# One cast and one low part for a weight block, in place of two halves of each

## The chip, the cores and the metric

The kernel runs on one NeuronCore of one Trainium2 chip. The metric is the device time of one execution in microseconds (us); the time before is the median of three runs.

## The reference

Two transformer blocks with two layers each, one after the other, on 256 tokens of width 1024, all in fp32. Cut to what matters here:

```python
def token_mixers(x, ...):                       # first block, per layer
    h = x @ w_in                                # 1024 -> 5704 columns, split into 11 parts
    ya = diff_attention(...)                    # 4 heads, two softmaxes each
    yb = dsa_attention(..., topk=64)            # 8 heads over the 64 best keys of an index
    merged = sigmoid(ga) * (ya @ w_bd) + sigmoid(gb) * (yb @ w_bs)
    return merged @ w_o
def first_block(...):
    x = layer_norm(ALPHA * x + mix)
    ffn = hierarchical_moe(x, ...)              # 32 experts, 2 of a group of 8 per token
    x = layer_norm(ALPHA * x + ffn + sigmoid(x @ w_ple_gate) * (p @ w_ple))
def second_block(...):                          # per layer
    x = x + hybrid_mixer(rms_norm(x) @ w_in)    # MLA, MoBA and retention branches
    x = x + square(relu(rms_norm(x) @ w_up)) @ w_down      # 1024 -> 4096 -> 1024
```

## The kernel before

The products outside the experts are made with split operands. Every weight block W (128 partitions by up to 2048 fp32 columns, 1 MB) becomes a pair: hi, which is W rounded to fp32r, and lo = W - hi. TensorE then makes three products for one, hi by hi, hi by lo and lo by hi (`mm3`, L1215, or `mm_both`, L1220). The experts' weights are used raw, with no pair.

A planner (`Plan`, L102) writes one list of steps, and each engine's program walks that same list and issues its own share of every step, in that order. So the order within an engine's queue is the plan's, and an instruction that waits holds up all that stand behind it on its engine. The steps that matter:

- `fetch` (L1186, the sync engine's queue): loads a block into a buffer, one of three ring buffers or one lent by other tiles. Where the buffer held a block that had been split, it waits for that block's low part.
- `split` (planned in `prepare`, L191): the block is made into its pair in one of three pairs of tiles WS (`PAIRS`, L46). ScalarE casts the high part, L2276, in two halves of the columns; before each it waits for the load and for TensorE to have read the pair's last block, three blocks earlier. VectorE makes the low part, L1638, in two halves, each behind its half of the cast. `ahead` (L184) plans a block's split up to two blocks before its use.
- Six of the 218 split blocks are marked "hi" (`low_part`, L570, L459, L557): their casts stay in their place, and each half of the low part is a step of its own further back. These are one in the second attention, one ahead of the first layer norm and one after the last expert, in each layer of the first block.
- `wide`, `gate`, `branch`, `mlp_up`, `mlp_down` and the like use one block each. TensorE waits for its whole low part (`lo_done`) and for a free PSUM bank; four banks go round, and ScalarE or VectorE frees each by an eviction or an addition. Such evictions are L2307 (ScalarE), L1837 and L1917 (VectorE). L2307 stands behind the casts in ScalarE's queue, L1837 and L1917 behind the low parts in VectorE's.

The steps around the prediction's places: `attend` (L315) orders an attention, whose scores L1794 to L1798 (VectorE) and exponentials L2334 (ScalarE) are mixed with blocks; `turn` (L251, TensorE's L1311) transposes heads; `turn_p` (L356, TensorE's L1382) transposes probabilities; `index` steps (L1771 to L1781) pick the 64 best keys on VectorE between the low parts; `route` steps on VectorE and ScalarE pick the experts and end in the mask MK (L2065), from which `ranks` (L1445) counts on TensorE. In the second block `rms`, `normed` and `wide` begin a layer, and `mlp_up` is relu, square and a correction that goes over VectorE (L2210), ScalarE (L2524, L2527), GpSimd (L2595) and VectorE (L2214).

Of the kernel before, what the change touches and what calls it, by code (L numbers as in the profile page):

```python
# [818 lines left out]
def build(nc, plan, table, wts, rows, cols, consts, pos, x0, x0T, pT, out):  # L819

    ctx = ExitStack()
    with ctx:
# [746 lines left out]
        def blocks_free(m):  # L1569

            return plan.split_block[m - PAIRS] if m >= PAIRS else None

        @block.vector
        def vector_program(e):
# [51 lines left out]
            for s in plan.steps:  # L1626
                l, i, u, t = s.l, s.i, s.u, s.t
                if s.kind == "split" and s.c != "hi":
                    hi, lo = WS[s.m % PAIRS]
                    buf = buffers[s.buffer]  # L1630
                    for k in range(2) if s.c is None else [s.c]:
                        c = slice(k * (s.n // 2), s.n // 2 if k == 0 else s.n)
                        dve.wait_ge(hi_done, "half", i, k)
                        if blocks_free(s.m) is not None:
                            dve.wait_ge(pe_done, "read", blocks_free(s.m))
                        if s.m in plan.also:
                            dve.wait_ge(pe_done, *plan.also[s.m])
                        nc.vector.tensor_tensor(lo[:, c], buf[:, c], hi[:, c].bitcast(F32), ALU.subtract).then_inc(  # L1638
                            *lo_done.inc(("block", i)))
# [225 lines left out]
                elif s.kind in ("turn_split", "shifted_split"):  # L1865
                    hi, lo = (v[:, 2 * s.j:2 * s.j + s.n, :] for v in SPLIT[s.name][0])
                    names = [(s.name, l, s.j)] + ([("x", l + 1, s.j)] if s.name == "ln2" else [("attn", l, s.j)] if s.name == "at0" else [])
                    if s.name in SHIFTED:
                        scale, bias = SHIFTED[s.name]
                        Y = (TMP, TMP2)[s.j % 2][:, 0:s.n * S]  # L1870
                        if s.kind == "turn_split":
# [6 lines left out]
                            for k in range(s.n):  # L1878
                                c = 2 * s.j + k
# [121 lines left out]
                elif s.kind == "route":  # L2001
# [51 lines left out]
                    elif n in (25, 27):  # L2053
                        c = (n - 25) // 2
                        nc.vector.tensor_tensor(val[:, c, t:t + 1], r_["m9"][:, c:c + 1], r_["es"], ALU.mult).then_inc(*dve_done.inc(name))
                    else:
                        c = (n - 26) // 2
# [191 lines left out]
        def scalar_program(e):  # L2249
# [15 lines left out]
            for s in plan.steps:  # L2265
                l, i, u, t = s.l, s.i, s.u, s.t
                if s.kind == "split" and s.c in (None, "hi"):
                    hi = WS[s.m % PAIRS][0]
                    for k in range(2):
                        c = slice(k * (s.n // 2), s.n // 2 if k == 0 else s.n)  # L2270
                        act.wait_ge(landed[s.buffer], "block", i)
                        if blocks_free(s.m) is not None:
                            act.wait_ge(pe_done, "read", blocks_free(s.m))
                        if s.m in plan.also:
                            act.wait_ge(pe_done, *plan.also[s.m])
                        nc.scalar.copy(hi[:, c], buffers[s.buffer][:, c]).then_inc(*hi_done.inc(("half", i, k)))  # L2276
# [83 lines left out]
                elif s.kind in ("turn_split", "shifted_split"):  # L2360
                    hi = SPLIT[s.name][0][0][:, 2 * s.j:2 * s.j + s.n, :]
                    name = (s.name, l, s.j)
                    if s.name in SHIFTED:
# [4 lines left out]
                        if s.kind == "turn_split":  # L2368
# [6 lines left out]
                            for k in range(s.n):  # L2375
                                c = 2 * s.j + k
# [298 lines left out]
```

## Time and profile before

| | |
|---|---|
| median of three runs | 1809.89 us (1809.01 to 1810.49) |
| profiled execution | 1810.35 us, span 1808.5 us |
| TensorE busy | 1776.3 us, 98% |
| VectorE busy | 1120.0 us, 62%, 2063 instructions |
| ScalarE busy | 860.5 us, 48%, 1515 instructions |
| low parts, L1638, out of the ring buffers | 460.7 us in 404 instructions |
| casts, L2276, out of the ring buffers | 390.3 us in 404 instructions |
| granted TensorE clock | 0.996 of full speed |

The profile is of one execution; the span runs from its first to its last instruction. A row of a timeline has the start, the duration, the engine, the line, the operation, the tile written and the tiles read with their sizes, and how many instructions are merged into the row; in square brackets is how long the engine was idle before it and what ended that. PE is TensorE, DVE VectorE, ACT ScalarE. WSh and WSl are the high and the low part of a block. Durations of neighbours overlap a little.

### The profile page before, as it was taken

What the parts mean: (1) busy time and instruction counts of PE and PEld (TensorE: products, weight loads), DVE (VectorE), ACT (ScalarE), POOL (GpSimd) and SP (SyncE); (2) the same over time, 40 slices, a digit from 0 to 9 for tenths busy, and PEclk for the clock granted to TensorE, in tenths of its full rate; (3) what the DMA queues carried; (4) which work ended last, traced back from release to release, by engine and by line L of the source; (5) the groups of instructions that cost most, each with busy time, mean ns of one, the idle gap of its engine ahead of it and who ended that gap; (6) DMA issues with size and microseconds to landing.
All of it is one profiled execution on the core that took longest, in us unless ns stands there. A gap on an engine that the chain in (4) does not pass through costs nothing.

```text
span 1808.5 us, 28658 instructions
## 1 busy us (share of the span) xinstructions
PE 1776.3 (98%) x11788; PEld 1444.6 (80%) x11788; DVE 1120.0 (62%) x2063; ACT 860.5 (48%) x1515; POOL 68.9 (4%) x79
## 2 busy tenths in 40 slices
PE   9999999999899999999989999999999999999998
PEld 8889975555688999555558899988888899988887
DVE  6986863233678777423347776775557577675555
ACT  5565542232545546223235655455554565455554
POOL 2000000000000000000000000001100000000001
PEclk9999999999999999999999999999999999999999
DMA  8427589999543576999975433545554533355552
GB/s 304 167 108 298 196 318 420 420 421 421 221 167 118 211 303 214 421 421 421 420 295 192 140 139 142 180 169 190 196 192 157 198 136 141 140 186 186 190 195 82
DMA packets 61083, 426.66 MB, mean 236 GB/s; under 512 B 6976, under 2 KB 7120, under 8 KB 11920
## 3 DMA queue, kind: packets, MB, share of 16 engines
q1 hardware_dynamic: 59760, 421.65, 61.3%
q8 instruction: 96, 1.57, 0.3%
q0 software_dynamic: 464, 1.89, 0.3%
q10 hardware_dynamic: 720, 1.19, 0.2%
q14 instruction: 43, 0.35, 0.1%
HBM read 423.66 MB, written 1.05 MB: 235 GB/s over the span
## 4 chain that ended last, share of the span: by engine, by line
PE 82%; DVE 12%; ACT 4%; issue 1%; POOL 1%; DMA 0%; DVEq 0%; POOLq 0%
PE bank L1213 64%; PE scp L1213 14%; DVE WSl L1638 4%; ACT SC L2334 2%; PE bank L1502 1%; DVE sm L1796 1%; PE bank L1343 1%; PE bank L1311 1%; DVE scp L1794 1%; ACT WSh L2276 1%; POOL sm L2549 1%; PE bank L1382 1%; DVE TMP L1781 0%; DVE sm L1587 0%; DMA A<-x0T 0%
## 5 line engine op out<-in xcount | busy, mean ns | idle before, releaser
L1638 DVE TENSOR_TENSOR WSl<-ring,WSh 128x1024 fp32r<-128x1024 f32 (+4 forms) x404 | 460.7, 1183 | 147.5 <-ACT WSh L2276 147.1
L2276 ACT CAST WSh<-ring 128x1024 fp32r<-128x1024 f32 (+4 forms) x404 | 390.3, 1020 | 160.6 <-PE scp L1213 80.4
L1213 PE MATMUL bank<-XB,WSh 128*128 128x256 f32 (+1 forms) x1920 | 433.1, 314 | 0.0
L1213 PE MATMUL bank<-XB,WSl 128*128 128x256 f32 x1216 | 331.7, 281 | 0.0
L1213 PEld LDWEIGHTS bank<-XB,WSh 128*128 128x128 f32 x1920 | 311.3, 191 | 19.4 <-issue 0.9
L1213 PE MATMUL bank<-WSh,XB 128*128 128x512 f32 (+4 forms) x1088 | 312.8, 367 | 5.3 <-DVE WSl L1638 3.6
L1213 PEld LDWEIGHTS bank<-XB,WSl 128*128 128x128 f32 x1216 | 231.5, 190 | 6.5 <-DVE XB L1902 0.6
L1213 PEld LDWEIGHTS bank<-WSh,XB 128*128 128x128 f32 x1088 | 199.2, 189 | 35.8 <-DVE WSl L1638 5.0
L1213 PE MATMUL bank<-WSl,XB 128*128 128x512 f32 (+4 forms) x544 | 198.7, 365 | 0.0
L1213 PE MATMUL scp<-WSh,FA 128*128 128x512 f32 x512 | 159.1, 389 | 0.0
L1213 PE MATMUL bank<-FA,WSh 128*128 128x256 f32 x640 | 116.6, 284 | 0.7 <-DVE FA L1846 0.7
L2152 DVE TENSOR_SCALAR WSl<-O,CST 128x256 fp32r<-128x256 f32 x64 | 22.3, 349 | 150.6 <-PE scp L1213 150.6
L1213 PEld LDWEIGHTS bank<-WSl,XB 128*128 128x128 f32 x544 | 102.9, 189 | 13.3
L1213 PEld LDWEIGHTS scp<-WSh,FA 128*128 128x128 f32 x512 | 96.1, 188 | 19.7
L2479 ACT COPY WSF<-bank 128x256 f32<-128x256 f32 x64 | 23.9, 373 | 171.9 <-PE bank L1213 171.9
L1213 PEld LDWEIGHTS bank<-FA,WSh 128*128 128x128 f32 x640 | 99.6, 192 | 1.7 <-issue 1.7
L1213 PE MATMUL scp<-WSl,FA 128*128 128x512 f32 x256 | 99.6, 389 | 0.0
L1213 PE MATMUL bank<-WSh,FA 128*128 128x512 f32 (+1 forms) x336 | 94.8, 365 | 0.0
L1213 PE MATMUL bank<-FA,WSl 128*128 128x256 f32 x320 | 90.5, 283 | 0.0
L1213 PE MATMUL bank<-A,WSF 128*64 128x256 f32 x672 | 76.4, 381 | 0.0
L2334 ACT ACTIVATE SC<-scp,sm 128x256 f32<-128x256 f32 (+1 forms) x128 | 52.2, 420 | 49.6 <-DVE sm L1798 48.9
L2549 POOL TENSOR_TENSOR sm<-sm,CST 128x1 f32<-128x1 f32 (+1 forms) x30 | 23.3, 780 | 1233.7 <-DVE sm L1606 1015.5
(325 smaller groups left out, 2445.2 us busy)
## 6 DMA issues: line engine op xcount, KB each, us to landing
ring<-wts SPq DMA_DIRECT2D x220, 1024.0 KB, 4.8
A<-wts SPq DMA_DIRECT2D x64, 1024.0 KB, 14.4
V<-wts SPq DMA_DIRECT2D x28, 1024.0 KB, 15.8
WSF<-wts SPq DMA_DIRECT2D x20, 1024.0 KB, 16.7
SC<-wts SPq DMA_DIRECT2D x16, 1024.0 KB, 16.0
PT<-wts SPq DMA_DIRECT2D x14, 1024.0 KB, 16.2
H<-wts SPq DMA_DIRECT2D x12, 1024.0 KB, 17.5
FAF<-wts SPq DMA_DIRECT2D x8, 1024.0 KB, 10.6
```

The lines of the kernel that those rows point to most:

```text
L1213: return nc.tensor.matmul(dst, lhsT, rhs, start=start, stop=stop)
L1311: last = nc.tensor.transpose(bank[u % 4][0:s.w, j * P:(j + 1) * P], src, ident)
L1343: last = nc.tensor.transpose(bank[u % 4][:, j * P:(j + 1) * P], src(t, c), ident)
L1382: last = nc.tensor.transpose(bank[u % 4][:, (j - s.first) * P:(j - s.first + 1) * P], p_at(j // nk)[:, j % nk * P:(j % nk + 1) * P], ident)
L1502: last = nc.tensor.transpose(bank[u % 4][:, f * P:(f + 1) * P], SE[s.e % 2][:, f * P:(f + 1) * P], ident)
L1638: nc.vector.tensor_tensor(lo[:, c], buf[:, c], hi[:, c].bitcast(F32), ALU.subtract).then_inc(*lo_done.inc(("block", i)))
L1794: nc.vector.tensor_tensor(v, v, mask.unsqueeze(1).broadcast_to([P, 4, kl - m0]), ALU.add).then_inc(*dve_done.inc())
L2152: nc.vector.tensor_scalar(ct, SR[:, 0, :], sid, None, ALU.is_equal).then_inc(*dve_done.inc())
L2276: nc.scalar.copy(hi[:, c], buffers[s.buffer][:, c]).then_inc(*hi_done.inc(("half", i, k)))
L2334: ins = nc.scalar.activation(SC[:, h, 0:kl], scp[:, h, 0:kl], ACT.Exp, bias=nb[t][:, h:h + 1], scale=SCALE[s.name], accum_out=zs[t][:, h:h ...
L2479: nc.scalar.copy(SE[s.e % 2], bank[u % 4][:, 0:DE]).then_inc(*act_done.inc(("bank", u), ("SE", l, s.e)))
L2549: nc.gpsimd.tensor_tensor(var, var, const("nhalf")[:, 0:groups], ALU.pow).then_inc(*pool_done.inc(("pow", *name)))
```

## The change

Where a split is not marked, one cast covers all columns of the block and one low part follows it. The signal that is left is that of the second half, k = 1. Marked splits keep their halves.

```diff
@@ vector_program
                 if s.kind == "split" and s.c != "hi":
                     hi, lo = WS[s.m % PAIRS]
                     buf = buffers[s.buffer]
-                    for k in range(2) if s.c is None else [s.c]:
-                        c = slice(k * (s.n // 2), s.n // 2 if k == 0 else s.n)
+                    for k in [1] if s.c is None else [s.c]:
+                        c = slice(0, s.n) if s.c is None else slice(k * (s.n // 2), s.n // 2 if k == 0 else s.n)
                         dve.wait_ge(hi_done, "half", i, k)
@@ scalar_program
                 if s.kind == "split" and s.c in (None, "hi"):
                     hi = WS[s.m % PAIRS][0]
-                    for k in range(2):
-                        c = slice(k * (s.n // 2), s.n // 2 if k == 0 else s.n)
+                    for k in [1] if s.c is None else range(2):
+                        c = slice(0, s.n) if s.c is None else slice(k * (s.n // 2), s.n // 2 if k == 0 else s.n)
                         act.wait_ge(landed[s.buffer], "block", i)
```

## Rows read from the trace of the kernel before

**Rows 1.** The page's busy time: us, share of the span, instructions.
```profile
PE 1776.3 (98%) x11788; PEld 1444.6 (80%) x11788; DVE 1120.0 (62%) x2063; ACT 860.5 (48%) x1515; POOL 68.9 (4%) x79
```

**Rows 2.** Groups by line and form: busy us, mean ns | idle before, releaser.
```profile
L2276 ACT CAST WSh<-ring 128x1024 fp32r<-128x1024 f32 x360 | 359.3, 1053 | 145.8 <-PE scp L1213 73.2 <-PE bank L1213 69.9 <-DMA ring<-wts 2.7
...
L2276 ACT CAST WSh<-ring 128x512 fp32r<-128x512 f32 x4 | 2.3, 618 | 5.6 <-PE bank L1213 5.6
...
L1638 DVE TENSOR_TENSOR WSl<-ring,WSh 128x1024 fp32r<-128x1024 f32 x360 | 424.9, 1223 | 135.4 <-ACT WSh L2276 135.2
...
L1638 DVE TENSOR_TENSOR WSl<-ring,WSh 128x512 fp32r<-128x512 f32 x4 | 2.6, 688 | 4.5 <-ACT WSh L2276 4.5
```

**Rows 3.** Timeline of 60 to 95 us: start us, us, engine, line.
```profile
63.74 1.99 ACT L2276 CAST WSh<-ring 128x1024 fp32r<-128x1024 f32 x2
...
64.81 2.36 DVE L1638 TENSOR_TENSOR WSl<-ring,WSh 128x1024 fp32r<-128x1024 f32 x2 [0.46 <-ACT WSh L2276]
...
84.47 1.99 ACT L2276 CAST WSh<-ring 128x1024 fp32r<-128x1024 f32 x2
...
85.67 2.35 DVE L1638 TENSOR_TENSOR WSl<-ring,WSh 128x1024 fp32r<-128x1024 f32 x2
...
92.15 1.97 PE L1311 MATMUL bank<-CST,A 128*128 128x128 f32 x16 [0.71 <-DVE A L1837]
```

**Rows 4.** Timeline of 128 to 152 us.
```profile
128.25 2.01 ACT L2276 CAST WSh<-ring 128x1024 fp32r<-128x1024 f32 x2
...
129.34 2.36 DVE L1638 TENSOR_TENSOR WSl<-ring,WSh 128x1024 fp32r<-128x1024 f32 x2
...
143.06 3.93 ACT L2276 CAST WSh<-ring 128x1024 fp32r<-128x1024 f32 x4
...
144.17 2.36 DVE L1638 TENSOR_TENSOR WSl<-ring,WSh 128x1024 fp32r<-128x1024 f32 x2
...
149.52 0.66 PE L1382 MATMUL bank<-CST,SC 128*128 128x128 f32 x4 [0.19 <-DVE H L1917]
```

**Rows 5.** Timeline of 218 to 240 us, the router.
```profile
220.92 1.69 DVE L1638 TENSOR_TENSOR WSl<-PT,WSh 128x704 fp32r<-128x704 f32 x2
...
227.92 1.45 ACT L2276 CAST WSh<-ring 128x704 fp32r<-128x704 f32 x2
...
228.72 1.69 DVE L1638 TENSOR_TENSOR WSl<-ring,WSh 128x704 fp32r<-128x704 f32 x2
...
232.85 1.45 ACT L2276 CAST WSh<-ring 128x704 fp32r<-128x704 f32 x2
...
233.65 1.70 DVE L1638 TENSOR_TENSOR WSl<-ring,WSh 128x704 fp32r<-128x704 f32 x2 [0.24 <-ACT WSh L2276]
...
237.12 0.23 DVE L2065 TENSOR_TENSOR MK<-OH 128x64 f32<-128x64 f32 x1
...
237.64 1.20 PE L1213 MATMUL bank<-MK,CST 128*128 128x32 f32 x10
```

**Rows 6.** Timeline of 946 to 982 us, where the second block begins.
```profile
946.65 1.68 ACT L2276 CAST WSh<-ring 128x832 fp32r<-128x832 f32 x2
...
968.39 2.36 DVE L1638 TENSOR_TENSOR WSl<-ring,WSh 128x1024 fp32r<-128x1024 f32 x2 [0.88 <-ACT WSh L2276]
...
980.09 1.25 ACT L2307 ACTIVATE A<-bank,sm 128x512 f32<-128x512 f32 x2
...
980.91 0.47 PE L1213 MATMUL bank<-WSh,XB 128*128 128x512 f32 x1 [1.50 <-DVE WSl L1638]
```

**Rows 7.** Low parts (L1638) in a stretch: VectorE's busy us, count, clock, DMA.
```profile
60.00:150.00 90.00, 27.19 (x24) 1.00 0.41 138
```

**Rows 8.** Timeline of 1210 to 1217 us, the second block's MLP.
```profile
1210.73 1.99 ACT L2276 CAST WSh<-ring 128x1024 fp32r<-128x1024 f32 x2
...
1211.93 2.35 DVE L1638 TENSOR_TENSOR WSl<-ring,WSh 128x1024 fp32r<-128x1024 f32 x2
...
1216.33 1.98 ACT L2276 CAST WSh<-ring 128x1024 fp32r<-128x1024 f32 x2
```

## The prediction

> **What bounds the kernel now.** I read the engines' busy time first, then the costs by line and form, then the waits of TensorE, then the timeline around each of them. TensorE is busy for 98% of the span [rows 1], so two of every hundred microseconds are all that any shortening can win; the question is rather what the change can add. The casts (ScalarE, L2276) and low parts (VectorE, L1638) are large groups, and TensorE hardly ever waits for either of them. VectorE, however, stands idle for 135.2 us in front of low parts because the cast isn't there yet [rows 2]. Most of that costs nothing, since a block is made two blocks ahead of its use. It costs where TensorE waits for something that stands *behind* a low part in VectorE's queue, or behind a cast in ScalarE's. The reader is to see four such places: 92.15, 149.52, 237.64 and 980.91 us [rows 3 to 6]. In the first two VectorE has run without a gap for tens of microseconds (scores, index search and low parts) and TensorE follows it.
>
> **What one instruction costs in place of two.** The cast takes 0.618 us for 512 columns and 1.053 us for 1024 [rows 2], so 0.85 ns a column over a fixed 0.18 us; 2048 columns, which no row of a cast shows, come to 1.053 + 2 x 0.435 = 1.92 us. The low part takes 0.688 and 1.223 us [rows 2], so 2048 columns come to 1.223 + 2 x 0.535 = 2.29 us. Bounds: at least the same slope with nothing fixed (1.74 and 2.14 us), at most twice a half (2.11 and 2.45 us); I take the straight line, since two sizes of the same instruction lie on it. Two consequences:
> - Busy time. A pair of low halves lasts 2.36 us [rows 3], so the second starts 1.14 us after the first, and what follows can start 2.28 us after the pair's start. A whole one lets it start after about 2.29 - 0.08 = 2.21 us. Gain 0.07 us a block on VectorE, and by the same reckoning 0.08 us on ScalarE. 212 of the 218 blocks are changed; the six that the plan marks "hi" keep halves.
> - Delay. VectorE starts when the whole cast is done, not the half: 1.92 - 1.05 = 0.87 us later. The whole block is ready 0.80 us later than now, wherever VectorE was waiting for ScalarE.
>
> The Trainium skill, page "VectorE: DVE Perf Modes", section on the TRN2 errata, says that the latency of SBUF is exposed between instructions, that a large tile pays it once and small tiles each time. That speaks for the change. The rows show that of the 0.15 us fixed in a low part 0.07 is left once neighbours overlap. By the page's rule alone the sum would be a gain (the third rival).
>
> **Part by part.** Each delay is followed from the cast to the wait of TensorE; "+" is later than now.
> - *First attention, to 92.15 us.* The cast starts at 63.74 and VectorE waits for its first half, starting at 64.81 [rows 3]. The whole cast ends at 65.66, the low part starts at 65.69: +0.88 - 0.07 = +0.81. Three further blocks, whose casts are long done, take back 0.07 each: +0.60. At 85.67 VectorE would arrive at 86.27, but the cast from 84.47 ends at 86.39 [rows 3]: start 86.42, +0.75, less 0.07 = +0.68. VectorE has no gap after this up to the copy that TensorE waits for at 92.15, where it has already waited 0.71. So 0.68 us arrive in full.
> - *Second attention, to 149.52 us.* The blocks before 128 us win and lose a tenth each: 0. The cast from 128.25 ends at 130.17, the low part starts at 130.20 and not 129.34 [rows 4]: +0.86 - 0.07 = +0.79; the block after it wins 0.07: +0.72. These 0.72 go through the softmax to ScalarE, whose cast of 143.06 starts at 143.78 and ends at 145.70; the low part of 144.17 starts at 145.73 [rows 4]: +1.56 - 0.07 = +1.49. Behind it stand the branch's additions that free the bank TensorE wants at 149.52, where it waits already. 1.49 us arrive.
> - *Router, to 237.64 us.* These blocks have 1408 columns: cast 1.38 us whole, 0.78 halved. The low part of 220.92 follows its half-cast at once [rows 5], so +0.60 - 0.07 = +0.53. One block with its cast done: +0.46. The routing steps between them feed each other over ScalarE, so the cast of 227.92 starts at 228.38 and ends at 229.76: low part at 229.79 for 228.72, +1.07 - 0.07 = +1.00. The cast of 232.85 starts at 233.85, ends at 235.23: low part at 235.26 for 233.65, +1.61 - 0.07 = +1.54 [rows 5]. The mask of 237.12 is then done at 238.89, and TensorE's ranks begin at 238.94 in place of 237.64: 1.30 us. Here TensorE does not wait today; its cover is 0.29 us (237.35 to 237.64), and it is used up.
> - The same three come again in the second layer of the first block (its rows repeat these, and TensorE waits at the same two): 2 x (0.68 + 1.49 + 1.30) = 6.9 us.
> - *Entry of the second block, to 980.91 us.* A block of 1664 columns: cast whole 1.60 us from 946.65, where a half is done at 947.54 [rows 6]: +0.71 - 0.07 = +0.64. Three blocks with their casts done: +0.43. At 968.39 VectorE waits for ScalarE, whose cast hangs on VectorE's own statistics: +0.43 + 0.87 - 0.07 = +1.23. This goes to ScalarE over the norms; two whole casts in its queue win 0.16, and the eviction of 980.09 comes 1.07 us later. The profile puts TensorE's wait at 980.91 down to the low part, but that eviction's first half ends at about 980.8, and the next product needs its bank. I add 1.1 us.
> - Start, the later attentions, the MLP's entries: each wins or loses a few tenths (gains where a wait of TensorE stands behind casts already started, losses of some 0.3 before the MLP); together 0, give or take 1 us.
>
> Sum: 6.9 + 1.1 = 8.0 us. Nothing else moves: no DMA is issued by the changed steps. Buffers are given back when the low part is done, 0.8 us later at most, under the cover of blocks fetched ahead. The profiled execution took 1810.35 us (span 1808.5), so 1818.4; the median of the runs shown is 0.5 lower, 1809.89, and its sum 1817.9. I say 1818.0.
>
> **Rivals.**
> - *Only part of the delays arrive* (3 to 5 us, about 1814). A gap in VectorE's queue that I took for full, or a whole low part nearer to the lower bound, would eat 0.2 to 0.4 us at each of the seven places. For it: the router's place depends on 0.29 us of cover and a long path. Against it: three kinds of place wait already.
> - *The delays are covered, and the shorter busy time decides* (not slower). Mechanism: VectorE comes to a low part so late that the whole cast is done; from 0.87 us after the end of a half cast on, a place wins 0.07 instead of losing 0.8. In 60 to 150 us there are twelve blocks, 24 halves [rows 7]; if all were such, 12 x 0.07 = 0.84 us a layer, 1.7 in two, and a few tenths of cast time in the second block: -2.3 us, 1807.6. For it: eight or so of those twelve are such. Against it: [rows 3, 4] show the four in each layer that are not, and [rows 5] three more behind them.
> - *The whole fixed term is saved*: 0.15 us on VectorE for each of those 24 blocks and no delay: -3.6 us and more, 1806. It is what the page's rule would do here. Against it is the 1.14 us spacing within the pairs.
> - *The MLP loses its cover* (far slower). In an up block ScalarE's cast starts only after the relu of the block before, which hangs on a correction behind the low part. From the low part's start at 1211.93 to the next cast is 4.4 us, casts being 5.6 apart, like TensorE's blocks [rows 8]. Whole: 1.92 + 0.03 + 4.4 - 0.07 = 6.3 us a turn, so ScalarE and VectorE fall back 0.7 us a block, 2.8 in four, and recover in the four down blocks. A block is finished two blocks, some 5.5 us each, before its use with one block to spare, so I cost it at nothing; without that cover it would be up to 2.7 us in each of eight quarters, some +21 us, 1839.
> - *The change does not do what it says*: excluded, as both loops are rewritten and the signal of the half that is left keeps its name.
>
> **How the numbers follow.** The forecast (1815.5 to 1821) has 0.60, the partial case (1812 to 1815.5) 0.19, covered 0.13, whole fixed term 0.03, MLP or another new wait 0.05. A measurement of this kernel can tell 0.2%, 3.6 us. Slower by more: 0.60 + 0.05 and most of the partial case, 0.80; within: the covered case and the rest of the partial one, 0.16; faster: 0.04, the third rival and the lucky end of the second. The range 1811.5 to 1821.5 leaves out the covered case and the large one.
>
> **What would show it.** After: 212 fewer instructions on each engine, casts of 1.92 and low parts of 2.29 us; VectorE's idle time before low parts up by most of 0.87 us for each wait; TensorE's wait at 92 us 1.4 in place of 0.7, at 149 us 1.7 in place of 0.2, a new one of 1.3 before the ranks, one of 2 to 2.6 near 981. I am wrong if TensorE's waits there haven't grown, or if a low part lasts under 2.1 us. If waits appear in the MLP, that rival holds.

## The result, and the profile after

The changed kernel takes 1821.43 us (median of four executions, 1820.13 to 1825.36), the kernel before beside it 1810.19, so 11.2 us more. The ratio of the two kernels is 1.0067, 95% interval 1.0055 to 1.0079, which is 12.1 us. In a second session it took 1821.23 against 1809.09 us, again 12.1 more. The direction was forecast; the size, 8 us, was too small. By the median the result lies just inside the range that was given (to 1821.5), by the ratio, 1822.0, just outside.

The profiled execution took 1820.13 us (span 1818.3 us), 9.8 us over the profiled one of before. First the page's busy times and the groups of the two changed instructions (as [rows 1] and [rows 2] have them).

```profile
PE 1778.1 (98%) x11788; PEld 1445.5 (79%) x11788; DVE 1106.0 (61%) x1851; ACT 840.4 (46%) x1303; POOL 70.2 (4%) x79
```

```profile
L1638 DVE TENSOR_TENSOR WSl<-ring,WSh 128x2048 fp32r<-128x2048 f32 x178 | 408.2, 2302 | 186.2 <-ACT WSh L2276 185.6
L2276 ACT CAST WSh<-ring 128x2048 fp32r<-128x2048 f32 x178 | 338.5, 1910 | 136.2 <-PE bank L1213 68.2 <-PE scp L1213 63.5 <-DMA ring<-wts 4.5
```

Each engine has 212 instructions fewer, the whole cast takes 1.91 us and the whole low part 2.30: the straight line through the two shorter forms held (1.92 and 2.29). VectorE is busy 14 us less, ScalarE 20 us less, and the kernel is slower. The group's idle time, waiting for casts, is 185.6 us in 178 instructions where it was 135.2 in 360. The next rows are of the timeline after, at the places of [rows 3, 4, 5]: ScalarE and VectorE at the first, then TensorE at each.

```profile
63.40 1.90 ACT L2276 CAST WSh<-ring 128x2048 fp32r<-128x2048 f32 x1
...
65.33 2.29 DVE L1638 TENSOR_TENSOR WSl<-ring,WSh 128x2048 fp32r<-128x2048 f32 x1 [0.95 <-ACT WSh L2276]
...
92.48 0.77 PE L1311 MATMUL bank<-CST,A 128*128 128x128 f32 x5 [1.38 <-DVE A L1837]
...
149.09 1.16 PE L1382 MATMUL bank<-CST,SC 128*128 128x128 f32 x8 [0.51 <-DVE H L1917]
151.33 0.92 PE L1382 MATMUL bank<-CST,SC 128*128 128x128 f32 x5 [1.08 <-DVE H L1917]
...
240.68 1.30 PE L1213 MATMUL bank<-MK,CST 128*128 128x32 f32 x10 [1.07 <-DVE MK L2065]
```

The low part now starts 1.93 us after its cast's start, and 1.07 before [rows 3]. TensorE's waits in the first block are near the forecast ones: 1.38 us at the first attention (1.4), 0.51 and 1.08 at the second (1.7 together), 1.07 before the ranks (1.3). The reader can follow the loss through the positions of the same matmul in both traces:

| TensorE's matmul | before | after | later by | this place's own share | forecast |
|---|---|---|---|---|---|
| after the start | 47.00 | 46.70 | -0.30 | -0.30 | 0 |
| first attention, layer 1 | 92.15 | 92.48 | 0.33 | 0.63 | 0.68 |
| second attention | 149.52 | 151.33 | 1.81 | 1.48 | 1.49 |
| router's ranks | 237.64 | 240.68 | 3.04 | 1.23 | 1.30 |
| end of layer 2 | 937.01 | 943.36 | 6.35 | 3.31 | 3.47 |
| entry of the second block | 980.91 | 989.39 | 8.48 | 2.13 | 1.1 |
| the blocks right behind it | 999.71 | 1009.67 | 9.96 | 1.48 | 0 |
| end of the span | 1808.5 | 1818.3 | 9.8 | -0.2 | 0 |

Down to the end of layer 2 the working holds within 0.6 us. The 0.30 us at the start are not the change's: in e4 and e12 below, whose first blocks are split as in the kernel before, the same matmul comes at 46.66 and 46.83 us. So from 47 us on the changed kernel loses 10.05 us. The two shares that it lacks are both at the entry of the second block. Here are the timelines there, after (VectorE, GpSimd, ScalarE and TensorE, in order of time), and then GpSimd's power before:

```profile
971.97 2.29 DVE L1638 TENSOR_TENSOR WSl<-ring,WSh 128x2048 fp32r<-128x2048 f32 x1
...
972.12 2.54 POOL L2549 TENSOR_TENSOR sm<-sm,CST 128x1 f32<-128x1 f32 x1 [1.45 <-DVE sm L1606]
...
974.70 0.61 ACT L2307 ACTIVATE A<-bank,sm 128x416 f32<-128x416 f32 x1 [3.38 <-POOL sm L2549]
975.21 1.90 ACT L2276 CAST WSh<-ring 128x2048 fp32r<-128x2048 f32 x1
...
977.13 2.29 DVE L1638 TENSOR_TENSOR WSl<-ring,WSh 128x2048 fp32r<-128x2048 f32 x1 [2.88 <-ACT WSh L2276]
...
988.57 1.25 ACT L2307 ACTIVATE A<-bank,sm 128x512 f32<-128x512 f32 x2
...
989.39 0.77 PE L1213 MATMUL bank<-WSh,XB 128*128 128x512 f32 x1 [3.20 <-ACT A L2307]
```

```profile
965.31 1.48 POOL L2549 TENSOR_TENSOR sm<-sm,CST 128x1 f32<-128x1 f32 x1 [1.45 <-DVE sm L1606]
```

GpSimd raises a variance of one column to the power -1/2. That takes 0.54 to 0.63 us where VectorE runs only short instructions, 1.48 beside two low halves, 2.54 beside one whole low part. The two long ones end about 0.4 us after the VectorE instruction that had started just before them. The same happens in the second layer of this block (1.47 us at 1382.59 before, 2.53 at 1392.58 after), where it costs TensorE nothing. At the entry ScalarE's eviction waits for the power, and the next cast stands behind the eviction in its queue: 1.06 us more. The releaser that the profile now names for the wait at 989.39 is the eviction L2307, as the prediction had read it against the profile of before.

The second share is TensorE's clock. These are windows of 20 us behind that wait, before and after; the column after the busy times is the granted clock.

```profile
981.00:1001.00 20.00, 19.55 (x114) 17.24 (x115) 11.62 (x20) 12.86 (x31) 0.00 (x0) 1.00 0.67 234
```

```profile
989.00:1009.00 20.00, 19.61 (x107) 17.31 (x108) 10.67 (x16) 11.02 (x16) 0.00 (x0) 0.91 0.59 194
```

Behind the wait of 3.20 us TensorE is granted half speed (1.2 in place of 2.4 GHz) for 3.4 us, and the same matmuls take 20.28 us (989.39 to 1009.67) where they took 18.80 (980.91 to 999.71): 1.48 us.

In the MLP the cast of an up block comes 6.12 us after the last one (5.59 before), ScalarE catches up in the down blocks, and TensorE loses only 0.2 us at each of the MLP's two entries, and wins as much elsewhere.

```profile
1221.24 1.90 ACT L2276 CAST WSh<-ring 128x2048 fp32r<-128x2048 f32 x1
1227.36 1.89 ACT L2276 CAST WSh<-ring 128x2048 fp32r<-128x2048 f32 x1
...
1240.72 1.91 ACT L2276 CAST WSh<-ring 128x2048 fp32r<-128x2048 f32 x1 [3.52 <-PE scp L1213]
```

That explains the 9.8 us of one execution. The medians differ by 11.2 and 12.1 us, and single executions of the changed kernel reach from 1819.2 to 1825.4 us. Why is asked below.

### The profile page after: what moved, and what is told of

Read it like the earlier page. It is cut to its first block, busy times and chain, and to the rows that moved or that the text cites. A ratio compares the mean times of both kernels' runs of the same rounds, so it can differ in the third digit from the quotient of the medians.

```text
span 1818.3 us, 28234 instructions
## 1 busy us (share of the span) xinstructions
PE 1778.1 (98%) x11788; PEld 1445.5 (79%) x11788; DVE 1106.0 (61%) x1851; ACT 840.4 (46%) x1303; POOL 70.2 (4%) x79
## 4 chain that ended last, share of the span: by engine, by line
PE 82%; DVE 10%; ACT 5%; issue 1%; POOL 1%; DMA 0%; DVEq 0%; POOLq 0%; ACTq 0%
PE bank L1213 65%; PE scp L1213 14%; DVE WSl L1638 3%; ACT WSh L2276 2%; ACT SC L2334 1%; PE bank L1502 1%; DVE sm L1796 1%; PE bank L1311 1%; DVE scp L1794 1%; PE bank L1343 1%; PE bank L1382 1%; POOL sm L2549 1%; DVE XB L1902 0%; DMA A<-x0T 0%; ACT XB L2393 0%
## 5 line engine op out<-in xcount | busy, mean ns | idle before, releaser
L1638 DVE TENSOR_TENSOR WSl<-ring,WSh 128x2048 fp32r<-128x2048 f32 (+5 forms) x206 | 447.4, 2180 | 203.3 <-ACT WSh L2276 202.8
L2276 ACT CAST WSh<-ring 128x2048 fp32r<-128x2048 f32 (+5 forms) x206 | 371.3, 1814 | 152.8 <-PE bank L1213 75.7
```

## The experiments

Blocks are numbered in the order in which they are split. All kernels but the filled ones and the repeat of the changed kernel are the kernel before with the number of pieces made a function of the block's number. A low part waits for the piece of its cast that ends it:

```diff
-                    for k in range(2) if s.c is None else [s.c]:
-                        c = slice(k * (s.n // 2), s.n // 2 if k == 0 else s.n)
+                    for c, k in low_cuts(s):        # low_n(s.m) pieces; k: the last piece of the cast that it needs
                         dve.wait_ge(hi_done, "half", i, k)
...
-                    for k in range(2):
-                        c = slice(k * (s.n // 2), s.n // 2 if k == 0 else s.n)
+                    for c, k in cast_cuts(s):       # cast_n(s.m) pieces; 2 in marked splits
                         act.wait_ge(landed[s.buffer], "block", i)
```

In their traces the low part is L1653, the cast L2290 and the power L2563. The results, each against the kernel before run beside it (1809.1 to 1809.7 us):

| kernel | pieces | median us | over before | ratio, 95% interval |
|---|---|---|---|---|
| changed, again | 1 and 1 | 1821.23 | 12.1 | 1.0064 (1.0050 to 1.0078) |
| e1 | cast 1, low part 2 | 1825.05 | 15.4 | 1.0079 (1.0063 to 1.0096) |
| e2 | cast 2, low part 1 | 1827.60 | 17.9 | 1.0094 (1.0077 to 1.0111) |
| e3 | 2 at 43 blocks, else 1 | 1809.30 | -0.4 | 0.9998 (0.9988 to 1.0007) |
| e4 | 1 at the entry | 1812.84 | 3.2 | 1.0015 (1.0006 to 1.0025) |
| e9 | 1 at the attentions | 1813.47 | 3.8 | 1.0023 (1.0013 to 1.0033) |
| e10 | 1 at the router | 1816.29 | 6.6 | 1.0031 (1.0019 to 1.0044) |
| e11 | 4 at 43 blocks, else 2 | 1813.82 | 4.1 | 1.0022 (1.0013 to 1.0032) |
| e14 | 2 at the router, else 1 | 1818.25 | 8.8 | 1.0050 (1.0035 to 1.0064) |
| e6 | changed, wait at the entry filled | 1822.29 | 13.2 | 1.0071 (1.0058 to 1.0085) |
| e15 | changed, entry and ranks filled | 1819.31 | 9.8 | 1.0050 (1.0035 to 1.0064) |
| e13 | e10, waits at the ranks filled | 1814.49 | 5.0 | 1.0025 (1.0016 to 1.0034) |
| e5 | low part 1 at one block, else 2 | 1813.89 | 4.8 | a single execution |
| e8 | before, filled behind a branch | 1812.09 | 3.0 | 1.0014 (1.0005 to 1.0023) |
| e12 | before, filled ahead of the branch | 1810.00 | 0.3 | 1.0003 (0.9993 to 1.0012) |

### One of the two merges alone

`cast_n` is 1 and `low_n` is 2 for every block:

> Casts of 212 blocks whole, low parts in two halves, both of which now wait for the whole cast. Theory (a merged pair costs what its low part has to wait: half a cast where VectorE stands ready for it, paid where TensorE waits for that block): the waiting is all there, so the first block's terms stay (+6.4 us by the positions of the trace after, 943 us against 937). In the second block's entry the low part that GpSimd's power stands beside is two instructions again, so the power takes about 1.5 us and not 2.5, and the wait before the 989 us matmul shrinks from 3.2 to about 2.1 us. Total 1817.6 us if TensorE's clock then stays at full speed behind that wait, 1819.1 if it still falls. Rival (each of the two merges brings its own share, and they add): about 1815.8, half of the 11.2 us between 1810.2 and 1821.4.

`cast_n` is 2 and `low_n` is 1:

> Casts in two halves, low parts of 212 blocks whole, each waiting for the second half of its cast. Theory: the same wait as with both merged, the same long GpSimd power (2.5 us) and the same clock drop after it: 1821.4 us, within 1. Rival (shares that add): about 1815.8 us, so that this and the run with whole casts together make up the 11.2.

Neither merge alone costs less than both together, so shares that add are out. The wait for the whole cast is what both have in common. Each also keeps the dearer pair of instructions on one engine: at the first layer's ranks (less the difference at 47 us) e1 is 0.9 us and e2 0.7 us later than the changed kernel, and 12 blocks at 0.07 us would be 0.84 (an estimate). GpSimd's power follows the low part alone; the rows are e1's, then e2's, and under each TensorE's wait at the entry:

```profile
979.02 1.48 POOL L2563 TENSOR_TENSOR sm<-sm,CST 128x1 f32<-128x1 f32 x1 [1.45 <-DVE sm L1622]
...
995.30 0.47 PE L1213 MATMUL bank<-WSh,XB 128*128 128x512 f32 x1 [2.20 <-DVE WSl L1653]
```

```profile
979.09 2.54 POOL L2563 TENSOR_TENSOR sm<-sm,CST 128x1 f32<-128x1 f32 x1 [1.45 <-DVE sm L1622]
...
996.63 0.47 PE L1213 MATMUL bank<-WSh,XB 128*128 128x512 f32 x1 [3.42 <-ACT A L2321]
```

The waits came as expected (2.1 forecast, 2.20 found), the totals did not: both are about 6 us over this theory's. In e1 TensorE's clock has the larger part of it. Behind the ranks of both layers the clock falls for 6.8 us (the window shown is the first's), and the same matmuls take 22.2 and 22.1 us (243.88 to 266.04, 718.42 to 740.53) where they took 19.9:

```profile
242.00:262.00 20.00, 19.54 (x108) 16.48 (x109) 11.46 (x36) 8.75 (x14) 0.63 (x2) 0.83 0.63 242
```

e2's trace has windows at 0.84 (718 to 738 us) and 0.83 (622 to 632 us), and it is 1.5 us later than the changed kernel's from the first 15 us on.

### Where the cost sits

`cast_n` and `low_n` are 2 at the 43 blocks and 1 elsewhere; then the other way round at the entry alone:

> Whole cast and whole low part everywhere except at 43 blocks: those beside the two first attentions (10 to 22, 49 to 61), those before the router's ranks (35 to 38, 74 to 77) and the entry of the second block (79 to 87), which keep their halves. Theory: the cost sits at these places alone, so the time is that of the kernel before or up to 0.4 us under it (the start gained 0.3): 1809.8 to 1810.4 us. Rival (the cost is spread over the merged blocks by their number, 169 of 212 left): 1819 us.

> The other way round: halves everywhere, and whole cast and low part only in the 9 blocks at the entry of the second block (79 to 87). Theory now (half a cast waited, plus GpSimd's power held 1.06 us longer behind a whole low part, plus TensorE at half clock for 3.4 us after a 3.2 us wait): +3.6 us, 1813.8 us; the power at 965 us takes 2.5 us, the wait near 981 us becomes 3.2, the matmuls behind it show the lower clock. The term on record in the prediction: +1.1 us, 1811.3 us. Cost spread over merged blocks by number: +0.5, 1810.7 us.

With halves at the 43 blocks the other 169 merges are free: 1809.30 us, no difference from the kernel before. The cost sits at those places entirely, and the MLP's blocks are shown harmless. The entry alone costs 3.2 us. In its profiled execution (1811.07 us) TensorE waited 3.23 us and the clock behind it stayed full. The matmul at 937 us comes 1.48 us earlier than in the kernel before and the one at 981 us 0.68 later, so the entry cost 2.16 us and not 3.6; its other executions lie at 1811.1 to 1814.9 us. So half clock does not follow every wait of this length.

The two parts of the first block, each alone:

> Whole cast and low part only in the 26 blocks beside the first two attentions of both layers (10 to 22, 49 to 61), halves elsewhere. Theory (half a cast waited per place): the waits near 92 and 561 us grow to 1.38 and 0.95, two waits before the second attention come back as in the changed kernel; +2.1 us a layer, +4.2 in all, 1813.9 us. Terms on record: 0.68 + 1.49 a layer, +4.3. Spread over blocks by number (26 of 212): +1.4, 1811.1 us.

> Whole only in the 8 blocks ahead of the router's ranks (35 to 38, 74 to 77). Theory: a new wait of about 1.1 us before the ranks in each layer, +1.2 us a layer, +2.5 in all, 1812.2 us, and single executions 2 to 3 us over that where TensorE's clock falls behind the new wait near 240 or 714 us (as it did in the runs with whole casts and with filled wait). Term on record: 1.30 a layer, +2.6. Spread over blocks by number (8 of 212): +0.4, 1810.1 us.

The attentions behave as forecast: 3.8 us by the medians, and by positions 2.1 us in each layer. The router does not. By positions its new waits are worth 1.23 and 1.28 us, as forecast, but the kernel costs 6.6 us in place of 2.5. TensorE's two new waits in the trace, and the windows behind them:

```profile
240.05 1.19 PE L1213 MATMUL bank<-MK,CST 128*128 128x32 f32 x9 [1.07 <-DVE MK L2080]
...
709.85 1.30 PE L1213 MATMUL bank<-MK,CST 128*128 128x32 f32 x10 [1.06 <-DVE MK L2080]
```

```profile
243.00:253.00 10.00, 10.00 (x45) 9.11 (x44) 9.76 (x27) 4.45 (x8) 0.63 (x2) 0.83 0.50 193
711.00:721.00 10.00, 9.53 (x42) 8.96 (x42) 8.86 (x20) 1.76 (x4) 0.53 (x1) 0.66 0.60 252
```

From 242.03 to 263.35 and from 711.88 to 734.40 us it takes 1.5 and 2.6 us longer than the kernel before takes for the same matmuls. It wins 1.0 us back between 474 and 515 us, where the kernel before has half clock too, at the end of a layer. Of that stretch TensorE is idle for 1.8 us in e10 and for 0.9 in the kernel before. Its executions lie between 1813.3 us (mean clock 0.997) and 1817.3 us (0.992). The other way round, the changed kernel without these 8 merges:

> The changed kernel with the 8 blocks ahead of the ranks put back to halves. Theory (those 8 blocks are worth 2.5 us of waiting and, in many executions, a half-clock stretch or two): 1817.5 us, 3.5 to 4 under the changed kernel, of which 2.5 by the trace's positions. Rival (the ranks' wait is worth 2.5 us and no more): 1818.8 us. Cost by the number of blocks: 1820.9 us.

It is 3.0 us under the changed kernel (1818.25 against 1821.23, in different sessions). That is between the two numbers, and its executions spread from 1817.1 to 1820.5 us; by itself it doesn't settle how much of the 3 us is clock.

### GpSimd's power alone

`low_n(82)` is 1, everything else 2:

> The kernel before with one instruction fewer: block 82's low part is whole (its cast, finished 8 us earlier, keeps its halves). It starts at 965.15 us, just ahead of GpSimd's power. Theory (GpSimd's power ends only when the VectorE instruction that was running ends): the power takes 2.5 us where it took 1.48, ScalarE's eviction and the next cast come about 1.06 us later, and TensorE's wait before the matmul at 981 us grows from 1.50 to 2.5 us, so the positions behind it are 1.0 us later (more if the clock falls there). Rival (the longer power in the changed kernel came of something else, and one merged low part whose cast lies ready costs nothing): power 1.5 us, wait 1.50 us, positions unchanged within 0.1.

```profile
966.17 2.54 POOL L2563 TENSOR_TENSOR sm<-sm,CST 128x1 f32<-128x1 f32 x1 [1.45 <-DVE sm L1622]
...
982.84 0.47 PE L1213 MATMUL bank<-WSh,XB 128*128 128x512 f32 x1 [2.61 <-DVE WSl L1653]
```

One low part whose cast lies ready, merged, makes the wait 1.11 us longer (1.50 in [rows 6]). Between the matmuls at 947 and 981 us the trace is 1.07 us longer than that of before, as expected, and the stretch behind it, to 1003.23, takes 20.39 us for 18.80: the clock fell here behind 2.61 us. In all 1813.89 us in its single execution, of which 1.3 us were already lost at the start of the kernel, before anything that was changed.

The Trainium skill, page "SBUF — State Buffer", section "SBUF: two separate sides", says that VectorE and GpSimd take one pair of ports in turn and hold it for a whole instruction, also a VectorE instruction with two SBUF inputs against a GpSimd one that reads SBUF. The long powers in these traces agree with it: they end 0.4 us behind the VectorE instruction that had started first, be it a half (1.48 us) or a whole low part (2.54). That the second low half then waits for the power in turn is not visible: its pair lasts 2.36 us as elsewhere.

### Keeping TensorE at work in the waits

Matmuls that nobody reads go into a PSUM tile that is free, ahead of TensorE's wait:

```diff
+            def filler(dst, n):
+                pe.wait_ge(dve_done, "rows")
+                for _ in range(n):
+                    mm(dst, PICK[:, 0:1].broadcast_to([P, P]), PR[:, 0:256], True, True)
...
+                    if s.name == "mv" and s.h == 0 and l == 0:
...
+                        filler(scp[:, 0, :], 12)
                     pe.wait_ge(lo_done, "block", i)
```

> The changed kernel with 12 matmuls of 256 columns that nobody reads, put on TensorE just before its 3.2 us wait at the second block's entry (they write a PSUM tile that is free). By the same form's 0.25 us each they take 3.0 us of the wait, so the needed matmuls start where they did. Theory (the half clock behind 989 us comes of TensorE having waited 3.2 us): the half-clock stretch at 989 us is gone, the stretch from 989 to 1010 us takes 18.8 us and not 20.3, and the median is about 1 us under that of the changed kernel run beside it. Rival (the half clock comes at that time whatever TensorE does): no difference, or 0.5 us slower by the extra matmuls.

> The changed kernel again, unchanged, for the spread of its executions and as the partner of the filled one: median 1821.4 us within 0.5. If the clock is what differs between its executions, the longer ones have the lower mean clock, in steps of about 1.5 to 3 us a stretch, as 1820.13 (0.995) and 1825.36 (0.992) had.

The repeat took 1821.23 us (1819.20 to 1823.74), and its longer executions have the lower mean clock. Its profiled execution (1821.67 us) is the second trace of the changed kernel. The first 15 us tell the two apart; the windows are the first trace's, then the second's:

```profile
10.00:15.00 5.00, 4.76 (x35) 4.76 (x36) 3.89 (x4) 3.22 (x3) 0.00 (x0) 1.00 0.68 194
```

```profile
10.00:15.00 5.00, 4.64 (x23) 4.64 (x24) 4.01 (x4) 2.14 (x2) 0.00 (x0) 0.66 0.69 198
```

The second has its matmul of 46.70 us at 48.37, and from there to the end every position is 1.5 to 1.8 us later. The rest is alike: full clock behind both layers' ranks, half clock for 3.4 us behind the entry, 9.9 us lost from 47 us on (10.05 in the first).

The window behind the wait in the filled kernel:

```profile
993.00:1013.00 20.00, 19.43 (x113) 17.23 (x114) 12.26 (x17) 12.62 (x27) 0.00 (x0) 1.00 0.64 229
```

There the half clock is gone, and the stretch takes 18.68 us (expected 18.8), though the 12 matmuls took only 1.6 us of the wait and not 3.0. The median did not follow: 1822.29 against 1821.23 us. In the profiled execution the clock had fallen behind the ranks instead, where nothing was filled: from 242.74 to 265.37 us it took 22.6 us for the kernel before's 19.9, and it fell behind the second layer's ranks too. So the ranks were filled too, first in e10, then in the changed kernel with 24 matmuls at the entry:

```diff
                 elif s.kind == "ranks":
+                    bank_free(u)
+                    filler(bank[u % 4][:, 0:256], 7)
                     pe.wait_ge(dve_done, "chosen", l)
...
-                    bank_free(u)
```

> As the kernel with whole blocks only ahead of the router's ranks (1816.3 us), with 7 unread matmuls on TensorE in the new wait of 1.07 us before the ranks (12 of this form took 1.6 us, so 7 some 0.95). Theory (the 2.5 us of the waits are there, and the other 4 of the 6.6 measured are half clock that follows them): no half-clock stretch near 243 or 711 us in most executions, 1812.3 us, spread under 3 us. Rival (the waits alone bring the 6.6 us, or the clock falls there whatever TensorE does): 1816 us again.

> The changed kernel with unread matmuls in both kinds of new long wait: 7 before the ranks of each layer, 24 in the 3.2 us wait at the second block's entry. Theory (its 11.4 us over the kernel before are about 8.5 us of waiting and 3 of half clock behind the new waits): 1818.5 us, no half-clock stretch near 242, 714 or 989 us in the profiled execution. Rival (the half clock isn't due to these waits): 1821.3 us or over.

The changed kernel, filled at both kinds of place; the matmuls of TensorE, and the windows behind the second layer's ranks and the entry:

```profile
711.76 0.98 PE L1213 MATMUL bank<-PR,PICK 128*128 128x256 f32 x7
712.96 1.30 PE L1213 MATMUL bank<-MK,CST 128*128 128x32 f32 x10 [0.23 <-DVE MK L2075]
...
986.93 3.12 PE L1213 MATMUL scp<-PR,PICK 128*128 128x256 f32 x24
990.38 0.47 PE L1213 MATMUL bank<-WSh,XB 128*128 128x512 f32 x1 [0.32 <-ACT A L2317]
```

```profile
712.00:732.00 20.00, 19.30 (x127) 15.34 (x125) 12.78 (x43) 9.38 (x15) 0.63 (x2) 1.00 0.74 283
990.00:1010.00 20.00, 19.31 (x113) 17.09 (x113) 12.24 (x17) 12.61 (x26) 0.00 (x0) 1.00 0.65 229
```

All waits of the changed kernel are still there, TensorE only isn't idle in them, and the median is 1819.31 us: 1.9 us less, with executions from 1818.6 to 1819.5 where the changed kernel's go from 1819.2 to 1825.4. By the traces the needed matmuls at the ranks and the entry are released when they were. What differs is the clock: behind the entry e15 loses nothing where the changed kernel loses 1.48 us. Behind the ranks neither trace of the changed kernel had half clock, so there e15's windows show no gain. The intervals of the two ratios overlap. In e13 the same fillers took 1.8 of the 4 us that were to go: one of the two stretches stayed (0.91 behind the first layer's ranks, 1.00 behind the second's), behind the 0.24 and 0.47 us of waiting that were left.

How far do waits and half clock go together? The traces can be counted, with the ranks of two layers and one entry in each of the 17.

| TensorE's wait | half clock behind it |
|---|---|
| ranks, no new wait (before, e3, e4, e5, e8, e9, e11, e12, e14) | 1 of 18 |
| ranks, new wait of about 1.1 to 1.3 us (the changed kernel twice, e1, e2, e6, e10) | 7 of 12 |
| ranks, the same wait filled (e13, e15) | 1 of 4 |
| entry, 1.0 to 1.5 us (before, e3, e8, e9, e10, e11, e12, e13) | 0 of 8 |
| entry, 2.2 to 3.4 us (the changed kernel twice, e1, e2, e4, e5, e14) | 6 of 7 |
| entry, 3.2 us filled (e6, e15) | 0 of 2 |

The one fall without a new wait is e11's, at 241.3 us, behind 0.47 us of waiting that the kernel before has there too:

```profile
240.00:250.00 10.00, 9.55 (x43) 8.84 (x44) 9.51 (x21) 3.22 (x5) 0.62 (x2) 0.83 0.56 235
```

So a new wait makes the fall more likely, and is neither enough for it nor always needed.

### Two that did not win

Quarters in place of halves at the 43 blocks, and unread matmuls in the two 3 us waits that the kernel before already has, ahead of the second layer and of the second block:

> The other direction: casts and low parts in four quarters at the 43 places, halves elsewhere. Theory (the low part starts when the first piece of its cast is done, so quarters bring a block about 0.36 us earlier, while each engine pays about 0.15 us more a block): the waits of the kernel before at 92, 561 and 981 us shrink by 0.2 to 0.4 us each, about 1 us in all, 1808.7 us. If the price of an instruction decides instead (86 more pairs of cuts at 0.15 to 0.3 us): 1812 us or more.

```profile
92.39 0.87 PE L1311 MATMUL bank<-CST,A 128*128 128x128 f32 x6 [1.13 <-DVE A L1852]
...
129.86 2.49 DVE L1653 TENSOR_TENSOR WSl<-ring,WSh 128x512 fp32r<-128x512 f32 x4
```

The wait at 92 us grew from 0.71 to 1.13 us where it should have shrunk. VectorE wasn't standing ready: at 129.86 us there is no idle time before the quarters, so nothing was gained by an earlier first piece, and four pieces take 2.49 us where two took 2.36. The wait at the entry did shrink, from 1.50 to 0.97 us, but the blocks ahead of it had lost 0.4. By positions the quarters cost 1.0 to 1.1 us in each layer's attentions; another 1.5 us of this trace are the half clock behind the ranks, which the edit did not bring by a wait. In this kernel one, two and four pieces give 1821, 1810 and 1814 us (the last only at the 43 blocks).

> The kernel before with 10 such unread matmuls on TensorE ahead of the first transposes of the second layer and of the second block, where TensorE waits 3.05 and 3.60 us and its clock is half for 6.8 and 3.4 us afterwards. Theory (half clock follows TensorE's waiting): both half-clock stretches go or shrink, which gives back up to half of each, 3 + 1.5 us: 1805.5 us, and at least 1 us under the kernel before. Rival (the half clock comes whatever TensorE does, or the short waits around are enough for it): 1810 us, within 0.5.

> The kernel before with the 10 unread matmuls moved ahead of TensorE's branch before the layer's end, since in the earlier try they started only when the 3 us wait was over. If half clock follows TensorE's waiting and the matmuls now lie in the wait (470.0 to 472.5 us, 938.2 to 940.7), the half-clock stretches behind 474 and 942 us go: about 1806 us. If the branch holds them until the wait is over as before: 1812 us, as in the earlier try.

In the first the matmuls started at 472.81 us, when the wait was over: TensorE still had the branch of the overflow case ahead of them. They cost about 1.6 us at each place. The window of 470 to 490 us has a clock of 0.91 where before has 0.83, that of 935 to 955 us 0.91 as before, and in all the kernel is slower, 1812.09 us (1.0014, 1.0005 to 1.0023). Moved ahead of the branch they ran from 469.79 us, and the window behind has the clock at full, where before has 0.83:

```profile
470.00:490.00 20.00, 16.28 (x120) 15.23 (x120) 17.90 (x31) 14.00 (x23) 1.53 (x2) 1.00 0.48 169
```

```profile
470.00:490.00 20.00, 15.96 (x101) 15.43 (x100) 17.60 (x30) 12.91 (x22) 1.53 (x2) 0.83 0.49 169
```

That execution took 1808.73 us, and the stretch that is gone was worth 1.3 us in it (from 469 to 515 us). The one near 942 us stayed. The median is 1810.00 (1.0003, 0.9993 to 1.0012), and the slower executions, which have no trace, have mean clocks of 0.995 to 0.997 where this one has 0.998. The expected 4 us did not come. No version tried is measurably faster than the kernel before.

## Why the prediction was right in direction and short in size

- *Durations of the whole instructions, 212 instructions, busy gain of 0.07 and 0.08 us a block*: right (1.91 and 2.30 us; 14.0 and 20.1 us over 212 blocks are 0.07 and 0.09).
- *The delay of half a cast, arriving where VectorE or ScalarE ends TensorE's wait*: right in place and size in the first block. 0.63, 1.48 and 1.23 us against 0.68, 1.49 and 1.30; with the second layer 6.65 us against 6.9 once the 0.3 us of the start are left out. That the seven places hold the whole cost is shown by halves at the 43 blocks there (e3).
- *Start, later attentions, MLP together 0*: right, -0.2 us behind the entry; the start's -0.3 is not the change's. The rival of the MLP losing its cover fell: its casts did fall back 0.5 us a block, and recovered.
- *The rivals of covered delays and of the saved fixed term*: neither. The gain of shorter busy time is there, on engines that nobody waits for. The Trainium skill, page "VectorE: DVE Perf Modes", section on the TRN2 errata, counts a fixed cost once for each tile. VectorE's busy time agrees in direction, 14 us less, with about half of the fixed 0.15 us saved a block; the kernel's time went the other way.
- *The step that failed first: the 1.1 us at the entry of the second block, from "the eviction of 980.09 comes 1.07 us later"*. It followed VectorE's and ScalarE's queues alone and took GpSimd's power as it stood. The power ends with the VectorE instruction that runs beside it, so it became 1.06 us longer, and the term is 2.13 us, 1.07 and 1.06. One whole low part beside the power, and nothing else changed, brings 1.07 us of it (e5, a single execution). [rows 6] does not hold the power's 1.48 us beside its usual 0.56; that ratio was the warning.
- *The step that failed second: TensorE's waits were priced at their own length.* The sum had no term for the clock. In both traces of the changed kernel the clock falls behind the entry, 1.48 us in the first. In kernels with the same new waits before the ranks it falls there as well, 1.4 to 2.8 us at a time. Filling the waits brings 1.9 us back by the medians, with intervals that overlap.
- With both the sum is 6.35 + 2.13 + 1.48 - 0.2 = 9.8 us in the profiled execution, and the second trace has the same loss from 47 us on. The medians differ by 1.4 to 2.3 us more. That this is half clock in the other executions, behind the ranks or in the first 15 us, fits the mean clocks (0.992 in the 1825.36 us execution, 0.995 in the profiled one), but it is not shown: neither trace of the changed kernel has half clock behind the ranks. It also stays open what decides in which execution the clock falls behind a wait of 1 to 3 us.

## What to carry to other kernels

A piece boundary is not only an overhead: the first half of a cast is what the next engine starts on, so merging costs nearly half an instruction where that engine stands ready and TensorE's own wait hangs on it, and is free elsewhere; here 43 of 212 blocks carried all of it. Follow such a delay through every engine that it passes, GpSimd too, whose small operation can be held by a longer VectorE instruction beside it. And where TensorE is the bound, a new wait is priced at its length plus, in some executions, 1.4 to 2.8 us of half clock behind it.

## What was not expected of the hardware

- A GpSimd tensor_tensor of one column takes 0.54 to 0.63 us beside short VectorE instructions, 1.48 behind a 1.2 us VectorE tensor_tensor of two SBUF inputs, 2.54 behind one of 2.3 us, in all traces alike (1.48 in the kernel before, e1 and e3, 2.54 in the changed one, e2, e4 and e5).
- TensorE's half clock comes in stretches of 3.4 and 6.8 us. One of 3.4 us behind the entry or the ranks cost 1.4 to 1.6 us, one of 6.8 us behind the ranks 2.2 to 2.8. The Trainium skill, page "TensorE: Matmul & The Clock Gate", section "Terms", puts the penalty at about the half-clock time times one half, 1.7 and 3.4 us. The traces have less, and least where the stretch lies on a wait: that of 6.8 us near 474 us was worth 1.3 us by e12. At the entry of the changed kernel TensorE was busy for nearly all of the stretch, so why it cost less than 1.7 us there is not shown.
- The same wait of 3.2 us at the entry had the clock fall behind it in both traces of the changed kernel and not in that of e4. A wait of 1.07 us had it fall in e10 at 243 us and in neither trace of the changed kernel.
- Executions of one kernel also differ at the very start: TensorE's matmul at 47.0 us comes between 48.1 and 48.4 in seven of the 17 traces, with the clock low from about 11 to 15 us, 1.2 to 1.7 us that no change here touched.
